# Products with the reciprocals behind their loads, gate low halves four steps later, no early table load, x in six pieces

## What is computed

```
proj = rms_norm(h, norm_g) @ w_in          # 2048 -> 5376 columns, split into
                                           # qa fa ia ga | qb kb vb gb | uc gc
ya = rms_norm(hgrn2_mixer(qa, fa, ia))     # A: gated linear recurrence, 4 heads of 128
yb = swa_sink_attention(qb, kb, vb)        # B: window 128, 16 heads of 64 on 2 key heads,
                                           #    QK-norm, rotary, sinks, meta keys visible
yc = multiscale_pool(uc)                   # C: trailing means of 2, 4, 8, 16 minus the token
mixed = concat(ya * silu(ga), yb * silu(gb), yc * silu(gc))
h = h + mixed @ w_out                      # 2048 -> 2048
```

## Time and profile before

| | us |
|---|---|
| median of 3 executions (lowest, highest) | 1561.88 (1560.76, 1562.08) |
| the profiled execution: device time | 1559.15 |
| its span from first to last instruction | 1557.3 |
| TensorE busy in it | 1540.7 |
| VectorE busy | 947.4 |
| ScalarE busy | 646.9 |
| GpSimd busy | 196.9 |

### The profile page before, as it was taken

The page is one execution under the profiler, slowest core; times in us unless marked ns, Lnnn a source line. Parts: engine busy times, 40 slices in busy tenths (PEclk is TensorE's granted clock), DMA queues, the critical chain, the costliest instruction groups (busy, mean ns, idle before and its releaser), DMA issues.

```text
span 1557.3 us, 26363 instructions
## 1 busy us (share of the span) xinstructions
PE 1540.7 (99%) x10456; PEld 1423.1 (91%) x10456; DVE 947.4 (61%) x1829; ACT 646.9 (42%) x1291; POOL 196.9 (13%) x348
## 2 busy tenths in 40 slices
PE   8999999999999999999999999999999999999999
PEld 8999899999999999999998889888999878888888
DVE  6787687777678445334335776876787774442322
ACT  6776566622332323232235665666232342321211
POOL 0112664400000000000000006544000000000000
DMA  7222112122221223344342222112223122234442
GB/s 279 99 82 82 56 55 72 65 71 95 83 72 65 82 93 112 124 135 153 124 136 100 81 85 79 55 60 77 83 82 109 55 82 95 95 123 149 136 150 68
DMA packets 39307, 151.78 MB, mean 97 GB/s; under 512 B 5376, under 2 KB 14352, under 8 KB 24336
## 3 DMA queue, kind: packets, MB, share of 16 engines
q1 hardware_dynamic: 38752, 149.52, 28.7%
q10 hardware_dynamic: 432, 0.57, 0.1%
HBM read 141.22 MB, written 8.59 MB: 96 GB/s over the span
## 4 chain that ended last, share of the span: by engine, by line
PE 89%; DVE 4%; DMA 2%; SPq 1%; POOL 1%; issue 1%; ACT 1%; DVEq 0%; POOLq 0%; ACTq 0%
PE ps_gemm L1142 77%; PE ps_mix L1029 2%; PE ps_mix L948 2%; PE ps_mix L994 2%; PE ps_mix L962 2%; PE ps_gemm L909 1%; DMA x_in<-in_xT 1%; DMA a_rden<-rden 1%; PE ps_gemm L1103 1%; PE ps_gemm L896 1%; SPq L461 1%; PE ps_mix L896 1%; SPq L465 1%; PE ps_mix L990 1%; DVE w_lo L1214 1%
## 5 line engine op out<-in xcount | busy, mean ns | idle before, releaser
L1142 PE MATMUL ps_gemm<-x_hi,w_hi 128*128 128x264 f32 (+3 forms) x2176 | 542.2, 314 | 0.5 <-issue 0.5
L1142 PE MATMUL ps_gemm<-x_hi,w_lo 128*128 128x264 f32 (+3 forms) x2176 | 528.1, 307 | 0.0
L1142 PE MATMUL ps_gemm<-x_lo,w_hi 128*128 128x264 f32 (+3 forms) x2176 | 527.6, 307 | 0.0
L1142 PEld LDWEIGHTS ps_gemm<-x_hi,w_hi 128*128 128x128 f32 x2176 | 353.6, 189 | 20.0 <-issue 0.9
L1142 PEld LDWEIGHTS ps_gemm<-x_hi,w_lo 128*128 128x128 f32 x2176 | 352.1, 188 | 19.4
L1142 PEld LDWEIGHTS ps_gemm<-x_lo,w_hi 128*128 128x128 f32 x2176 | 351.5, 188 | 16.9
L645 ACT ACTIVATE w_hi<-w_stage 128x512 fp32r<-128x512 f32 x464 | 267.0, 618 | 169.5 <-DVE z L1307 122.7
L1214 DVE TENSOR_TENSOR w_lo<-w_stage,w_hi 128x512 fp32r<-128x512 f32 x392 | 256.8, 690 | 66.2 <-ACT w_hi L645 60.4
L1142 PE MATMUL ps_gemm<-mixed_hi,w_lo 128*128 128x264 f32 (+1 forms) x752 | 199.0, 320 | 0.0
L1142 PE MATMUL ps_gemm<-mixed_lo,w_hi 128*128 128x264 f32 (+1 forms) x752 | 198.7, 319 | 0.0
L1142 PE MATMUL ps_gemm<-mixed_hi,w_hi 128*128 128x264 f32 (+1 forms) x752 | 197.6, 318 | 0.0
(11 more groups left out here) (195 smaller groups left out, 1626.9 us busy)
## 6 DMA issues: line engine op xcount, KB each, us to landing
w_stage<-in_w_in SPq DMA_DIRECT2D x82, 1024.0 KB, 4.9
w_stage<-in_w_out SPq DMA_DIRECT2D x32, 1024.0 KB, 5.3
res<-in_xT SPq DMA_DIRECT2D x16, 264.0 KB, 5.3
h1T<-z SPq DMA_DIRECT2D x16, 264.0 KB, 5.7
res<-h1T SPq DMA_DIRECT2D x16, 264.0 KB, 5.3
a_rden<-rden SPq DMA_DIRECT2D x32, 128.0 KB, 4.9
out<-z SPq DMA_DIRECT2D x15, 256.0 KB, 5.6
x_in<-in_xT SPq DMA_DIRECT2D x2, 1056.0 KB, 13.7
```

Of the source, the lines that this page charges most:

```text
L1142: ins = pe.matmul(g[:, bank, 0:size], ws, xs[:, k, c:c + size], start=tick == 0 and i == 0, stop=tick == TICKS - 1 and i == 2)
```

## The change

Four edits, none of which adds or drops a matmul:

- RECIP_LOAD_SLOTS from (22, 26) to (22, 27): the second set of loads is issued a block later. RECIP_AT: the eight products leave block 23 tick 0, block 26 tick 11 and block 29 tick 0; two stand in block 23 (ticks 9, 11), one each in 25 and 26 (ticks 10, 9) for the first set, and (28, 10), (28, 14), (29, 9), (29, 11) for the second.
- gate_low moves from tick 5 to tick 9, there behind the tick's w_low. It does so for all 16 gates of both layers: four during the attention (blocks 15 to 18), twelve after it (31 to 42).
- The activation on eps_col, its semaphore and VectorE's wait for that are gone. The builder now puts the first ACT_TABLE_LOAD ahead of the first x_hi, behind that instruction's waits for x's first piece and for eps_done.
- x comes in six pieces: chunks 4 to 7 are one DMA of 1 MB instead of two of half a MB. The later pieces keep their places among the weights.

```diff
--- before.py
+++ after.py
@@ -44,6 +44,7 @@
 TICKS = KC
 HI_TICKS = (2, 5, 8, 11)
 HQ_TICK = 10
+GATE_LOW_TICK = 9
 
 
 MINI = {1: ("rms", 0)}
@@ -89,7 +90,7 @@
             yield N - n + c
 
 
-X_PIECES = ((0, 1), (1, 2), (2, 4), (4, 6), (6, 8), (8, 12), (12, 16))
+X_PIECES = ((0, 1), (1, 2), (2, 4), (4, 8), (8, 12), (12, 16))
 EARLY_SQUARES = {3: 0, 6: 1, 9: 2, 12: 3}
 N_EARLY = len(EARLY_SQUARES)
 SECOND_SKIPS = (3, 7, 11, 15)
@@ -122,8 +123,8 @@
 ATT_Q0 = [0, len(ATT_B[0])]
 
 
-RECIP_LOAD_SLOTS = (22, 26)
-RECIP_AT = ((23, 0), (23, 9), (23, 11), (25, 10), (26, 11), (28, 10), (28, 14), (29, 0))
+RECIP_LOAD_SLOTS = (22, 27)
+RECIP_AT = ((23, 9), (23, 11), (25, 10), (26, 9), (28, 10), (28, 14), (29, 9), (29, 11))
 
 
 def recip_loads(layer, rounds):
@@ -364,7 +365,7 @@
         s_res = [sem("res_in0"), sem("res_in1")]
         s_sto = [sem("store0"), sem("store1")]
         s_lb, s_eps = sem("lb_step"), sem("eps_done")
-        s_v, s_table = sem("vector_link"), sem("table_loaded")
+        s_v = sem("vector_link")
 
         def parts(c0, w):
 
@@ -478,11 +479,10 @@
             load_x(2)
             load_first_w(0, 4, 8, s_wq[0][1])
             load_x(3)
-            load_x(4)
             load_first_w(0, 8, 16, s_w[0])
             load_first_w(1, 8, 16, s_w[1])
+            load_x(4)
             load_x(5)
-            load_x(6)
             for N in range(NTOT):
                 layer, n = divmod(N, NC)
                 if N + 2 < NTOT:
@@ -665,9 +665,8 @@
             for c, q in ((1, 0), (1, 1)):
                 act.dma_start(wst[:, c, 4 * q:4 * q + 4].rearrange("p k c -> p (k c)"),
                               w_in[0, c, :, 4 * q * P:4 * (q + 1) * P]).then_inc(s_wq[c][q], 16)
+            act.wait_ge(s_prm0, 16)
             act.wait_ge(s_eps, 1)
-            act.activation(lbt[:, 0, 0:1], epsc[:, 0:1], ACT.Copy).then_inc(s_table, 1)
-            act.wait_ge(s_prm0, 16)
             for k in range(KC):
                 for i, (k0, _) in enumerate(X_PIECES):
                     if k == k0:
@@ -1260,7 +1259,6 @@
 
                 l0, l1 = prm_sb[:, 0, C_LB:C_LB + HA], prm_sb[:, 0, C_LB + HA:C_LB + 2 * HA]
                 link(dve.tensor_tensor(lbt[:, 4], l0, l1, ALU.max))
-                dve.wait_ge(s_table, 1)
                 link(dve.tensor_tensor(lbt[:, 0], l0, lbt[:, 4], ALU.subtract))
                 dve.tensor_tensor(lbt[:, 1], l1, lbt[:, 4], ALU.subtract).then_inc(s_lb, 1)
 
@@ -1704,7 +1702,7 @@
                         pooling_last(N - 1)
                     if tick - 1 in HI_TICKS and N + 1 < NTOT and not low_on_pool(N + 1) and N > 2:
                         w_low(N + 1, HI_TICKS.index(tick - 1))
-                    if tick == 5 and pkind == "gate":
+                    if tick == GATE_LOW_TICK and pkind == "gate":
                         gate_low(N - 1)
                     r = rope_at(layer, n, tick, 5)
                     if r is not None:
```

## The result

The changed kernel takes **1554.08 us** (median of 5 runs, 1553.84 to 1554.28), the kernel before 1562.08 us beside it (median of 5, 1560.76 to 1566.98). The ratio is 0.9945, 95% interval 0.9931 to 0.9959: about 8.0 us faster.

What follows compares the result with a forecast made beforehand. TensorE, busy 1540.7 of 1557.3 us, was taken as the bound, leaving 16.6 us of idle to win. The terms 1.45 + 2.18 + 1.16 - 0.15 = 4.64 us, taken from 1561.88, gave 1557.2 us; range 1555.7 to 1560.0.

Steps and rivals of the forecast that it cites:

- The anchor: Starting time 1561.88 us, median of three runs; its 2.7 us above the profiled execution was taken as untouched by the change.
- Product of block 23: Layer 0, head of block 23: moving the product to tick 9 ends TensorE's idle before the norm's matmul; 1.45 us gained.
- The spare 1.4 us: Block 23: the copy of head 0's output can come 2.8 us earlier, 1.4 us more than TensorE's wait needs.
- Product of block 26: Moving this product closes TensorE's waits in block 27 for h_vt (0.80 us) and h_qp (1.38 us); 2.18 us gained.
- The later loads: Second set issued in slot 27 instead of 26 still lands 10 us before its first product; zero effect.
- gate_low and h_k: Block 31, both layers: gate_low at tick 9 lets h_k updates start 0.74 us earlier, closing both transpose waits; 1.16 us gained.
- The start: Table load before first x_hi costs zero (at most 0.4 us); x in six pieces costs 0.15 us.
- Waits that only shrink: Rival: waits at block 27 and the gates shrink without closing, the start costs 0.45 us; 1559.0 us, chance 0.18.
- The slow start: Rival: TensorE's stretch at the lower clock after the start lasts twice its 2.6 us; 1557.9 us, chance 0.07.
- Half or all of the attention gates: Two rivals: gate_low costs 0.75 us at half of eight attention gates (1560.2 us, 0.08) or all (1563.3 us, 0.05).

## Why the prediction was wrong, step by step

**The anchor: failed.** "The median of the three runs, 1561.88, lies 2.7 above the profiled execution, which carries no part of the change" is the step that broke. The 2.7 us carried a great deal of it. Once the waits for a_rden are gone, the profiled execution and the median differ by 0.2 us (1554.28 and 1554.08); before, by 2.9. The terms that it left too small are the two of the products, 1.45 and 2.18 us. The gap was there to be read, with its sign: the profiled execution was shorter than every timed run, the kernel has three waits for a DMA whose landing varied from 4.0 to 7.7 us, and TensorE stood behind two of them. A sum from that execution could only be a lower bound for these terms.

**Product of block 23, 1.45 us: right mechanism, mis-sized.** Upper bound 1.45, since the wait was taken as known. It was 1.45, 2.56, 2.7, 2.0 and 2.1 us long in five traces that have it. Its price was 1.75 us even in the trace that the prediction read, 2.3 to 3.0 in three others and 3.9 where the clock fell behind it; as a part by itself it was worth 1.4 to 2.2 us in time. The spare 1.4 us that the prediction found is right: h_square_lo is early by 1.3.

**Product of block 26, 2.18 us: right mechanism, mis-sized, and the larger error.** Its price was 2.65 us in the trace of before, 2.9 to 3.5 in four others, 4.6 where the clock fell, and 3.2 to 4.1 us in time as a part by itself. Both together were worth 7.0 us in time against 3.63. In the traces with all three TensorE waits they cost 4.4 to 6.35 us; no such trace has the lower clock at a wait, and no profiled execution of one of the long runs exists. The prediction had no term for the clock at these waits. That its sum of 4.64 us lies so near the 4.8 us between the two profiled spans is in part luck: in them the waits for a_rden cost 4.4 us instead of 3.63, and those for h_k gave 0.5 of their 1.16.

**The later loads, zero: right.** Issued from 413.98, the first product of the second set at 442.12 waits for nothing.

**gate_low and h_k, 1.16 us: half wrong in its reason.** "Both waits close" failed: they went from 0.61 and 0.55 to 0.36 and 0.32 us, because what gate_low had stood behind was not the last thing in the row; the low half of tick 6 waits 0.51 us for w_hi. The time gained was nevertheless about this size: 0.7 to 1.2 us between the medians of the kernel with only the products and the changed one, which ran on different chips. The other part came in the attention, which had been put at zero with 0 to 6.0 us of loss: against the same matmuls, TensorE is 0.3 us earlier after blocks 18 and 19 of layer 0 and 0.2 us in layer 1's attention, in gaps too small to be listed as waits. One such place on VectorE, gate_low in the kernel before and in the changed one:

```profile
1020.36 1.66 DVE L1411 TENSOR_TENSOR mixed_lo<-z,mixed_hi 128x512 fp32r<-128x512 f32 x1
```

```profile
1019.79 0.69 DVE L1409 TENSOR_TENSOR mixed_lo<-z,mixed_hi 128x512 fp32r<-128x512 f32 x1
```

Why it took 1.66 us where it stood, and how much of the gain comes from there, is open.

**The start, 0.15 us lost: nothing.** The kernel with that part alone is at 1.0004 of before, 0.9995 to 1.0013. ScalarE's table load waits for x and the x_hi behind it:

```profile
3.97 1.28 ACT L651 ACT_TABLE_LOAD   x1 [3.97 <-DMA x_in<-in_xT]
...
5.27 0.73 ACT L651 ACTIVATE x_hi<-x_in,prm_sb 128x528 fp32r<-128x528 f32 x1
...
7.58 0.51 PE L908 MATMUL ps_gemm<-x_hi,w_hi 128*128 128x264 f32 x2 [2.32 <-DVE w_lo L1213]
```

x_hi starts 1.3 us later than in the earlier trace rows (foreseen 1.1), TensorE 0.5 us later, and the two idles of 0.47 and 0.25 us ahead of its later matmuls swallow it: the last matmuls of the first two blocks start at 32.88 us before and at 32.90 after. The activation again starts 0.02 us after the end of the load; a drain of 1.38 us, as the Trainium skill has it ("ScalarE: Activation LUTs", What ACT_TABLE_LOAD costs), shows here no more than before.

**The rivals.** Waits that only shrink: true of h_k alone (0.68 us left of 1.16). The slow start: the slow stretch was 3.4 us long, not twice 2.6, and cost nothing at the end of block 1 (in the earlier trace rows the slow pace lasted until 10.0, not 9.7 us). Half or all of the attention gates: no loss there. All four had been drawn from the structure of the kernel, none from the spread of its runs, and so none could end below 1555.7 us.

## What to carry to other kernels

Before a sum is made from a profiled execution, set its time against the timed runs: if it lies outside them, some wait in it has not its usual length, and a wait on a DMA that ends on the critical path is the first candidate; give its term an upper bound that includes the gap. The price of such a wait is not its length in the list of waits: measure it between two instructions that both kernels have, and look at the granted clock behind it. A chain of many small DMAs in one queue (16 issues of 0.6 us here) followed by a consumer on a shared engine was met here by distance: a consumer placed a block later cost nothing and took 7 us and the scatter with it. When an instruction is moved out of a row that holds up another engine, look at what is next in that row, and whether it itself waits.

## What the runs showed of the hardware that I had not expected

**The clock can fall at a wait of 1.4 to 2.1 us.** In two of the traces the granted clock went to 0.50, the lower level, for 3.3 and 3.4 us at a wait of TensorE, which cost 1.4 us on top of the wait; five other traces with such waits of 1.4 to 2.7 us show no fall.

**A load lands late because of the one behind it.** The last 4 KB load of the first set took 7.7 to 8.9 us from issue to landing where a 1 MB load was issued 1.1 to 1.4 us after it, and 5.3 us where that was held back; the loads of the set issued before 349 take 4.3 to 5.4.

**Issues in one queue are not of one length.** In the first row of sixteen every issue takes 0.6 to 0.7 us and the row 9.8 us in every trace that has sixteen; in the second, with a weight load ahead of it, it takes 10.2 to 11.8 us, with single issues of up to 1.8 us.

**The slow stretch at the start moves, and the record of the clock does not always show it.** The changed kernel by stretches of 2 us (us, busy (instructions) by engine, granted clock, DMA, GB/s):

```profile
8.00:10.00 2.00, 2.00 (x13) 2.00 (x13) 0.92 (x3) 1.30 (x2) 0.00 (x0) 0.66 1.04 364
10.00:12.00 2.00, 2.00 (x11) 2.00 (x10) 1.58 (x3) 1.50 (x3) 0.00 (x0) 0.50 0.99 414
12.00:14.00 2.00, 2.00 (x18) 2.00 (x18) 1.64 (x4) 1.72 (x4) 0.00 (x0) 0.99 1.04 425
```

The granted clock is 0.50, the lower level of 1.2 GHz, from 8.7 to 12.0 us, after TensorE had stood for 2.3 us and worked for 1.1; 11 matmuls are made where 18 are at the upper level. In the earlier trace rows the pace was the same and the clock read 1.00. By the pace of the matmuls the slow stretch began anywhere from 7.0 to 8.7 us and ended between 10.0 and 13.8 in the fourteen traces of this study. The two traces of the changed kernel end it at 12.0 and 12.8 us: that it varies from run to run of one kernel is what the Trainium skill says of the start ("TensorE: Matmul & The Clock Gate", HAM clock gate). The first norm's matmul, near 49 us, stands up to 1.0 us apart between traces; this stretch probably moves it, and is probably what is left of the scatter; neither is shown.
